# Expert rows gathered pair by pair, and an eighth weight slot asked for after the out-projection

## The reference, cut to what matters

```python
order = jnp.argsort(flat_e)                 # assignments sorted by expert
xs = x_pad[slot_tok].reshape(n_blocks, MOE_BLOCK, D)
def expert_block(args):
    xb, e = args
    return (jax.nn.silu(xb @ w_gate[e]) * (xb @ w_up[e])) @ w_down[e]
ys = lax.map(expert_block, (xs, block_e)).reshape(n_slots, D) * slot_w[:, None]
```

## Time and profile before

| | |
|---|---|
| median of three runs | 1631.71 us |
| the profiled execution | 1633.28 us |
| its span | 1631.5 us, mean granted TensorE clock 0.996 |
| busy: PE, VectorE, ScalarE, POOL | 1447.4, 605.4, 341.0, 245.7 us |
| HBM read, written | 461 MB, 47 MB |
| TensorE's wait for expert weights | 88.8 us |

### The profile page before, as it was taken

The page is one execution under the profiler, slowest core; times in us unless marked ns, Lnnn a source line. Parts: engine busy times, 40 slices in busy tenths (PEclk is TensorE's granted clock), DMA queues, the critical chain, the costliest instruction groups (busy, mean ns, idle before and its releaser), DMA issues.

```text
span 1631.5 us, 24179 instructions
## 1 busy us (share of the span) xinstructions
PE 1447.4 (89%) x8991; PEld 903.8 (55%) x8991; DVE 605.4 (37%) x1517; ACT 341.0 (21%) x983; POOL 245.7 (15%) x290
## 2 busy tenths in 40 slices
PE   8999999999999988787878999999999977777785
PEld 3655466655566655454555555655666655555453
DVE  2145677752532221222213556423522222222225
ACT  2122377741110000000001345412100000000000
POOL 1122100000211111111112233000211111111112
PEclk9999999999999999999999999999999999999998
DMA  7115140026689999999999501473899999999997
GB/s 289 51 52 206 52 155 1 2 115 235 246 340 428 429 429 429 429 430 429 429 429 422 201 1 78 181 297 116 334 390 428 429 429 427 429 431 429 429 430 296
DMA packets 44373, 480.67 MB, mean 295 GB/s; under 512 B 11034, under 2 KB 11562, under 8 KB 24656
## 3 DMA queue, kind: packets, MB, share of 16 engines
q1 hardware_dynamic: 28144, 450.17, 65.9%
q0 software_dynamic: 15008, 25.37, 4.4%
q10 hardware_dynamic: 1152, 4.19, 0.6%
HBM read 461.33 MB, written 47.19 MB: 312 GB/s over the span
## 4 chain that ended last, share of the span: by engine, by line
PE 58%; DMA 32%; DVE 6%; issue 2%; ACT 1%; DVEq 0%; another core or an unknown queue 0%; POOL 0%; SPq 0%
DMA sb_arena<-moe_w 32%; PE ps L1173 12%; PE ps L1368 7%; PE ps L1583 7%; PE ps L1182 6%; PE ps L1689 2%; PE ps L1719 2%; PE ps L1704 2%; PE ps L1549 2%; PE ps L1409 2%; PE ps L1437 2%; PE ps L1433 1%; PE ps L1490 1%; PE ps L1520 1%; PE ps L1617 1%
## 5 line engine op out<-in xcount | busy, mean ns | idle before, releaser
L1173 PE MATMUL ps<-sb_arena,sb_x_block 128*64 128x256 f32 x4096 | 472.6, 383 | 91.5 <-DMA sb_arena<-moe_w 88.8
L1173 PEld LDWEIGHTS ps<-sb_arena,sb_x_block 128*64 128x64 f32 x4096 | 419.1, 197 | 198.6 <-issue 130.6
L1182 PE MATMUL ps<-sb_arena,sb_hidden_space 128*64 128x512 f32 x1024 | 247.9, 605 | 44.1 <-ACT sb_hidden_space L898 44.1
L768 POOL DMA_INDIRECT expert_rows<-sb_y_sb,sb_row_now x124 | 132.5, 1069 | 746.5 <-DVE sb_y_sb L1955 642.5
L1954 DVE COPY sb_row_now<-sb_row_of 128x1 uint32 (+1 forms) x124 | 19.1, 154 | 598.2 <-PE ps L1182 588.2
L898 ACT COPY sb_hidden_space<-ps 128x128 f32<-128x128 f32 x128 | 34.2, 267 | 755.8 <-PE ps L1248 755.8
L1182 PEld LDWEIGHTS ps<-sb_arena,sb_hidden_space 128*64 128x64 f32 x1024 | 62.1, 136 | 141.2 <-issue 73.1
L1368 PE MATMUL ps<-sb_sorted_rows,sb_arena 128*128 128x512 f32 x256 | 114.6, 594 | 2.1 <-DVE sb_arena L2199 1.3
L1965 DVE TENSOR_TENSOR sb_x_block<-sb_sorted_rows,sb_moe_gain 128x512 f32<-128x512 f32 x124 | 85.9, 693 | 25.0 <-issue 20.7
L1955 DVE COPY sb_y_sb<-ps 128x512 f32<-128x512 f32 x124 | 84.4, 681 | 0.0
L1368 PEld LDWEIGHTS ps<-sb_sorted_rows,sb_arena 128*128 128x128 f32 x256 | 46.9, 190 | 51.4 <-issue 48.8
...
## 6 DMA issues: line engine op xcount, KB each, us to landing
...
kept_rows<-sb_arena SPq DMA_DIRECT2D x8, 512.0 KB, 4.9
token_rows<-sb_arena ACTq DMA_DIRECT2D x8, 512.0 KB, 2.7
```

The source lines that it names most:

```text
L768: pool.indirect_dma_start(out=ys_dram.rearrange("r (j n) -> (r j) n", j=2), out_offset=bass.IndirectOffsetOnAxis(ap=row_now[:, u:u + 1], a ...
L1173: last = nc.tensor.matmul(ps[j * BLOCK:(j + 1) * BLOCK, bank, 0:2 * P].rearrange("p (g n) -> p g n", g=2), x_rows[:, :, k], weights[:, 0:2 ...
L1182: last = nc.tensor.matmul(ps[j * BLOCK:(j + 1) * BLOCK, 2, :], hidT[:, c * BLOCK:(c + 1) * BLOCK], weights[:, 2, c * D + j * 512:c * D + ( ...
```

## The change

- `pair_rows` takes the place of `xsT`: two buffers of 128 rows. POOL gathers the rows of two experts with one indirect DMA of 128 rows of 4 KB (`gather`): partitions 0 to 63 are ranks 0 to 63 of the even expert, 64 to 127 those of the odd one. Places without a token get the number 1000, which is out of bounds and skipped. There are 32 such gathers in a layer in place of 8. Gather m + 2 waits until pair m is turned, and stands on POOL between the sends of pair m - 1 and those of pair m.
- TensorE turns each block (8 transposes of 64 rows, `turn_block`) just before the up-projection of the block ahead of it, and VectorE's `deal_block` reads the turned block from PSUM. The eight `turn_chunk` and the copies back fall away.
- The token table is made tile by tile: ranks within an expert (`read_ranks`, `mark_ranks`) and the inverse (`invert_tile`), so that after the last pick less is left to do. The sorted places (`pos`) follow later, and the tables for extra blocks (`extra_tables`) after the first two blocks are dealt.
- `sorted_rows` has room now: its first 24 KB are an eighth weight slot. SP asks for it whole, 3072 KB, when the out-projection is done (`out_done`), ahead of its wait for `last_rows_sent`. A slot is reloaded eight experts later, not seven.

The diff, cut to its core (helpers for extra blocks, semaphores and buffer names are left out):

```diff
-SLOTS = 7
+ARENA = 7
+SLOTS = ARENA + 1
...
-        arena = sb("arena", [P, SLOTS * SLOT])
+        arena = sb("arena", [P, ARENA * SLOT])
...
-        xsT = sorted_rows[:, :].rearrange("p (n k) -> p n k", k=KD)
+        pair_rows = sorted_rows[:, SLOT:SLOT + 2 * D].rearrange("p (i n) -> p i n", i=2)
...
+        def slot_space(l, u):
+
+            return places(l, u) if u < ARENA else sorted_rows[:, 0:SLOT]
+
...
@@ -566,6 +586,8 @@
                     if t == 1:
                         sp.wait_ge(first_rows_sent, 32 * (l + 1))
                         part(RING + 1, RING + 1, 0, 1).then_inc(weights_loaded[RING + 1], 16)
+                sp.wait_ge(out_done, OUT_PARTS * (l + 1))
+                expert_weights(sp, l, ARENA, ARENA).then_inc(weights_loaded[ARENA], 16)
                 sp.wait_ge(last_rows_sent, 32 * (l + 1))
                 sp.wait_ge(logits_done, TILES * (l + 1))
                 part(RING + 2, RING + 2, 1, 3).then_inc(weights_loaded[RING + 2], 16)
@@ -584,10 +606,7 @@
 
                         sp.wait_ge(down_done, (i - 1) * SLOTS + (done + u + 1))
                         expert_weights(sp, l, i * SLOTS + u, u).then_inc(weights_loaded[u], 16)
-                for n in range(EXPERTS // SLOTS * SLOTS, EXPERTS):
-                    sp.wait_ge(down_done, done + n - SLOTS + 1)
-                    expert_weights(sp, l, n, n % SLOTS).then_inc(weights_loaded[n % SLOTS], 16)
-                sp.wait_ge(down_done, done + EXPERTS // SLOTS * SLOTS - SLOTS + 2)
+                sp.wait_ge(down_done, done + EXPERTS - SLOTS + 2)
                 for t in range(TILES):
                     sp.dma_start(x_of[l + 1][:, t, :], x_dram[t * P:(t + 1) * P, :]).then_inc(x_loaded[t], 16)
 
...
             def moe_moves(l):
                 base = l * EXPERTS
+                def gather(pair, j, tokens):
+                    pool.indirect_dma_start(
+                        out=pair_rows[:, j, :], out_offset=None, in_=h_dram,
+                        in_offset=bass.IndirectOffsetOnAxis(ap=tokens, axis=0),
+                        bounds_check=S - 1, oob_is_err=False).then_inc(pair_landed[j], 16)
+
+                pool.wait_ge(out_done, OUT_PARTS * (l + 1))
+                step(pool.memset(pair_rows, 0.0))
                 pool.wait_ge(token_ready, l + 1)
                 pool.wait_ge(first_rows_sent, 32 * (l + 1))
                 pool.wait_ge(last_rows_sent, 32 * (l + 1))
-                for c in range(CHUNKS):
-                    pool.indirect_dma_start(
-                        out=xs_in(c), out_offset=None, in_=h_dram,
-                        in_offset=bass.IndirectOffsetOnAxis(ap=token_of[:, c:c + 1], axis=0)).then_inc(rows_landed[c], 16)
+                for j in range(2):
+                    gather(j, j, token_of[:, j:j + 1])
 
                 pool.wait_ge(tables_ready, l + 1)
                 for j in range(2):
@@ -761,15 +801,34 @@
 
                 if l == 0:
                     pool.wait_ge(rows_filled, 16 * (ROWS // S))
-                with pool.Fori(0, SENT_PAIRS) as i:
+                def send(i, u):
+                    pool.wait_ge(y_ready, i * 2 + (l * SENT + u + 1))
+                    pool.sem_inc(y_seen, 1)
+                    pool.indirect_dma_start(
+                        out=ys_dram.rearrange("r (j n) -> (r j) n", j=2),
+                        out_offset=bass.IndirectOffsetOnAxis(ap=row_now[:, u:u + 1], axis=0),
+                        in_=y_sb[:, u, :], in_offset=None, bounds_check=2 * ROWS - 1, oob_is_err=False
+                    ).then_inc(y_written[u], 16)
+
+                for j in range(2):
+                    pool.wait_ge(block_turned, base + 2 * j + 2)
+                    gather(j + 2, j, token_of[:, j + 2:j + 3])
                     for u in range(2):
-                        pool.wait_ge(y_ready, i * 2 + (l * SENT + u + 1))
+                        send(j, u)
+                step.enter(0, 2)
+                with pool.Fori(1, SENT_PAIRS // 2) as i:
+                    step.turn = i - 1
+                    for j in range(2):
+                        pool.wait_ge(block_turned, i * 4 + (base + 2 * j + 2))
                         pool.sem_inc(y_seen, 1)
-                        pool.indirect_dma_start(
-                            out=ys_dram.rearrange("r (j n) -> (r j) n", j=2),
-                            out_offset=bass.IndirectOffsetOnAxis(ap=row_now[:, u:u + 1], axis=0),
-                            in_=y_sb[:, u, :], in_offset=None, bounds_check=2 * ROWS - 1, oob_is_err=False
-                        ).then_inc(y_written[u], 16)
+                        step(pool.tensor_copy(token_now[:, j:j + 1], token_of[:, bass.ds(i * 2 + (j + 2), 1)]))
+                        pool.sem_inc(y_seen, 1)
+                        gather(i * 2 + j + 2, j, token_now[:, j:j + 1])
+                        for u in range(2):
+                            send(i * 2 + j, u)
+                step.leave(SENT_PAIRS // 2 - 1)
+                for u in range(2):
+                    send(SENT_PAIRS - 1, u)
...
+                nc.tensor.matmul(ranks_at(t), below[:, :], pick[:, 2, t, :], start=(t == 0), stop=True).then_inc(counted, 1)
+                if t == TILES - 1:
+                    nc.tensor.matmul(totals, ones[:, :], picks_until(t), start=True, stop=False)
+                    nc.tensor.matmul(totals, ones[:, :], pick[:, 2, t, :], start=False, stop=True)
+
+            def invert_tile(l, t):
+
+                pe.wait_ge(hots_ready, l * TILES + t + 1)
+                for k in range(TOPK):
+                    for j in range(2):
+                        last = nc.tensor.matmul(ps[j * BLOCK:(j + 1) * BLOCK, INVERSE_BANK, 0:EXPERTS // 2], rank_hot[:, t, k, :],
+                                                tokens_at[:, t, k, :].rearrange("p (e j) -> p j e", j=2)[:, j, :],
+                                                start=(t == 0 and k == 0), stop=(t == TILES - 1 and k == TOPK - 1))
+                return last
...
-                def turn_chunk(c):
-                    pe.wait_ge(rows_landed[c], 32 * l + 16)
-                    if c >= 2:
-                        pe.wait_ge(xsT_act, l * CHUNKS + c - 1)
-                        pe.wait_ge(xsT_dve, l * CHUNKS + c - 1)
+                def turn_rows(half, i, bank):
+                    rows_at = slice(half * BLOCK, (half + 1) * BLOCK)
                     for k in range(KD):
-                        for half in range(2):
-                            part = slice(half * BLOCK, (half + 1) * BLOCK)
-                            last = nc.tensor.transpose(
-                                ps[:, CHUNK_BANK + 2 * (c % 2) + half, :].rearrange("p (n k) -> p k n", k=KD)[:, k, :],
-                                xs_in(c)[part].rearrange("p (m k) -> p k m", k=KD)[:, k, :], ident[part, part])
-                    last.then_inc(chunk_turned, 1)
-
-                turn_chunk(0)
-                turn_chunk(1)
-                keep_busy(3)
+                        last = nc.tensor.transpose(
+                            ps[:, bank, :].rearrange("p (n k) -> p k n", k=KD)[:, k, :],
+                            pair_rows[rows_at, i, :].rearrange("p (m k) -> p k m", k=KD)[:, k, :], ident[rows_at, rows_at])
+                    return last
+
+                def turn_block(c, fours):
+                    half, i = c % 2, c // 2 % 2
+                    if half == 0:
+                        pe.wait_ge(pair_landed[i], (fours + (l * (EXPERTS // 4) + c // 4 + 1)) * 16)
+                        if not isinstance(fours, int):
+                            pe.sem_inc(y_seen, 1)
+                    turn_rows(half, i, TURN_BANK + half).then_inc(block_turned, 1)
+
+                turn_block(0, 0)
+                turn_block(1, 0)
+                keep_busy(1)
                 up(0, 0, 0)
-                turns = (SENT - FIRST) // turn
-                with pe.Fori(0, turns) as i:
-                    for c in range(FIRST, FIRST + turn):
-                        up(i * turn + (c + 1), c + 1, i * 2 + (c + 1) // SLOTS)
-                        down(i * turn + c, c)
-                for n in range(FIRST + turns * turn, SENT - 2):
+                for n in range(SLOTS):
+                    turn_block(n + 2, 0)
                     up(n + 1, n + 1, (n + 1) // SLOTS)
                     down(n, n)
-                n = SENT - 2
-                down(n, n)
-                up(n + 1, n + 1, (n + 1) // SLOTS)
-                down(n + 1, n + 1)
+                turns = (SENT - 2) // SLOTS
+                with pe.Fori(1, turns) as i:
+                    for c in range(SLOTS):
+                        turn_block(c + 2, i * 2)
+                        up(i * SLOTS + (c + 1), c + 1, i + (c + 1) // SLOTS)
+                        down(i * SLOTS + c, SLOTS + c)
+                for n in range(turns * SLOTS, SENT - 2):
+                    turn_block(n + 2, 0)
+                    up(n + 1, n + 1, (n + 1) // SLOTS)
+                    down(n, n)
```

(43 more changed lines are left out.)

281 lines of the change are left out of this document (141 added, 140 removed).

## The result

The changed kernel takes 1815.55 us (median of four runs, 1812.4 to 1826.39), the kernel before beside it 1631.56: a ratio of 1.1142 (95% interval 1.1098 to 1.1187), 184 us slower. The forecast was 1718, with a range from 1625 to 1775. The sign and the place were right, the size was short by more than half. The profiled execution took 1826.39 us, span 1824.2.

The account below looks back on a forecast made before the run. The kernel before was taken as bound by expert weights from HBM, the changed one by late gathers. Per layer 43.1 (loop) + 3.0 (rest) - 2.8 (start) = 43.3 us, 86.6 in both: 1718 us, range 1625 to 1775.

Parts of the forecast that it names:

- The bound: Expert loop: waits for weights give way to waits for gathers, 7.8 us per expert, +43.1 us per layer.
- L: Expert loop: time from the end of down-projection 2m - 1 until gather m + 2 has landed and TensorE starts, 18.3 us.
- The count of turns: DMA queues in the loop: send's 5 and gather's 9 packets per engine each wait for a 0.92 us weight packet.
- 3.2 of fixed time: Send under load: 7.8 us to land, less 4.6 us of packet turns, leaves 3.2 us of fixed cost.
- eight transposes at 0.44 us: TensorE's loop iteration: eight added transposes cost (1.98 - 1.10) / 2 = 0.44 us.
- 6.45: TensorE's own time per expert in the loop, in us: 6.01 + 0.44 for eight transposes.
- my own scale of 56 experts in two layers: Loop from the fourth expert on: each us of L costs 56 x 0.25 = 14 us per layer.
- the clock: Slower rival: TensorE's clock falls in the loop's stalls, 1.7 us lost in each, 1766 us in all; chance 0.12.
- The three terms: Loop cycle of four experts: L of 18.3 us plus two TensorE iterations, 12.9 us, with no clock loss.
- The start: Start of the expert phase in each layer: first up-projection earlier, -2.8 us, near 443.0; bounds -5 to +3.
- The faster rival: Loop gathers land in time (L under 14.7 us), weights bound the loop, -10 us per layer, 1612 us; chance 0.12.
- the 7.5 reckoned: Faster rival: eighth load fills the loss at the loop's start, 408 against 415.8 us, -7.5 per layer.

Follow-up runs that it names:

- the third experiment: Changed kernel, but TensorE turns both experts of a pair together, 16 transposes alternating between partitions 0 to 63 and 64 to 127: 1797.12 us, ratio 1.1014.

## Why the prediction was wrong

- **The bound, right.** The 88.8 us of waits for weights went, gathers that come late took their place, in both layers from about the ninth expert on (forecast: from the first blocks), and the eighth slot was worth nothing here. The change's own mechanism broke on the gathers' latency, as forecast.
- **L, right for the gathers that stall.** 18.8 us on average against 18.3. The count of turns (5 + 9 packets at 0.92) was borne out by the packet records and by the run with loads in thirds. In the gather shown, the send's first packet went 4.4 us after its issue (541.3 - 536.95), where 3.2 of fixed time had been reckoned. POOL's gap between send and gather was 2.1 us and not 1.1, but the gather's packets stood right behind the send's, so it cost nothing. What I had wrong is that every gather takes turns all the way: sixteen of the 28 in the loop of layer 0 landed within 10.6 us. That hardly moved the forecast, since a late gather in every second pair sets the pace.
- **The step that failed first: eight transposes at 0.44 us.** I took half the difference of two rows whose transposes alternate between the two halves of the partitions. Eight of one half have nothing to overlap with and take 1.02 of the iteration (535.11 to 536.13): 6.45 should have been 7.24. The pair of timeline rows in the third experiment shows it. In the chain this adds 1.6 us to four experts, by my own scale of 56 experts in two layers about 45 us. The Trainium skill, "TensorE: Matmul & The Clock Gate", section "The mechanism" of Part 3, says that loads of the array overlap with running products only where the row groups differ; the trace agrees (16 in 1.10 us, 8 in 1.03 to 1.09).
- **The step that failed next: the clock, put at 0.12 and left out of the sum.** Eleven of the twelve stalls of layer 0 were followed by an up-projection at the lower level, wholly or in part, 2.2 us a time on average (24.4 over eleven), against the 1.7 I had priced from mixer 1. Over all cycles this adds 1.9 us to four experts, about 53 us in all. I argued from waits of 1.2 us per expert that leave the clock alone, but the stalls I forecast did not look like these: forecast as 2 to 3 us per pair, they came as 5 us in every second pair.
- The three terms together, over four experts: forecast 18.3 + 12.9 = 31.2, measured 18.6 + 14.5 + 1.9 = 35.0, the mean of the nine cycles of layer 0 that have four experts from stall to stall. With the stretches in which all gathers were in time the mean is 34.0 (510.5 / 15).
- **The start, wrong in sign.** -2.8 forecast, +3.8 measured, outside even my bound of +3. The token numbers came as reckoned; the rows took 12 us instead of 2.7, and the run with the later request shows that the eighth slot's load was the cause. That they too take turns with 24 KB packets is likely, but not read from their packets; I had used that count for the gathers and not for them.
- **The faster rival** was wrong for this kernel and right in kind: with the gathers in time, the eighth slot is worth 7 us per layer against the 7.5 reckoned. But the rule for which I gave it a chance, that an engine drains some 9 to 17 descriptors before it changes queues (the Trainium skill, "DMA: Bandwidth & Descriptors", section "Queues, rings and completion order"), is not what these traces show. The packets of a gather with rows of 4 KB are single rows, and while both queues had work they changed nearly one for one (96 against 116 packets in 7 us, 135 against 135 in 3 us with runs of 8 KB). Where such a gather did land within 10 us, those looked at passed in a gap between two weight loads.

No version beats the kernel before. The best two, dealt ranks with loads in thirds or in halves, are 0.76% (0.59 to 0.93) and 0.73% (0.6 to 0.87) slower. Per layer the first wins 7 us by the slot and some 5 at the start (441.09 against 445.83), and pays 53 x 0.15 = 8 us for the gathered rows and 53 x 0.17 = 9 for the short runs.
